# Expert loop of a mixture-of-experts layer: token rows gathered from HBM in every pass, or picked from SBUF in every second one

## The chip, the cores and the metric

The kernel runs on one core of one Trainium2 chip. The metric is the device time of one execution in microseconds. TensorE, VectorE, ScalarE, GpSimd and SyncE are called PE, DVE, ACT, POOL and SP, as in the profile.

## What is computed

The program is a two-layer decoder trunk on 512 tokens of width 1024. Each layer has a token mixer (layer 0 a forgetting attention, layer 1 an RWKV-7 recurrence), beside it a cross-attention into a memory, and then a mixture of experts with a residual and a layer norm. The change touches only the mixture of experts, which runs once in each layer:

```python
scores = sigmoid(x2 @ w_router)
_, idx = top_k(scores + router_bias, 6)           # 6 of 64 experts for each of 512 tokens
gate = renormalised scores of those six * 2.5
for each expert e:                                # xb: the rows of x2 whose idx names e
    hb = silu(xb @ w_gate[e]) * (xb @ w_up[e])    # 1024 -> 256
    yb = hb @ w_down[e]                           # 256 -> 1024
    acc[tok] += yb * gate
```

So 3072 (token, expert) rows of 4 KB go through 64 experts, whose weights are 3 matrices of 1 MB each. Everything is float32.

## The kernel before, in words

`routed_experts_tables` computes the routing of a layer. It leaves in SBUF the rank of every token within every expert (`K.rank`), columns from which token numbers can be computed (`K.slot_cols`), and a plan: experts are taken two by two, a pair at a time, and each pair gets one pass with 64 slots for either expert, or more passes where an expert has more than 64 tokens. It also stores the layer's activations X (512 x 1024, which stay resident in SBUF too) to HBM as `x_rows` (L278).

`expert_loop` (from L468) is the loop over passes. Every engine runs its own loop; the bodies are written out for the pass numbers of even and odd parity (`u` or `s`, 0 and 1), since most buffers are double. The first two passes stand ahead of the loop (L524). What the engines do for pass n:

- DVE makes a one-hot matrix of token against slot in bfloat16, [128 tokens, 4 token tiles, 128 slots], by comparing ranks with slot numbers (`one_hot`, L532), four passes ahead.
- PE multiplies it with `slot_cols` (`slot_rows`, L540, three passes ahead), which gives the token number of each of the 128 slots. DVE turns it into an index column (`index_rows`, L550).
- POOL starts an indirect DMA, the gather, with that column. It brings 128 rows of 4 KB from `x_rows` into `xg[s]`; indexes of empty slots are out of bounds and move nothing (`gather`, L560). It is issued two passes ahead, once PE has turned the rows that were in the buffer.
- PE transposes the gathered rows in 8 blocks of 128x128, `turn_x` (L568), into banks 0 and 1. ACT and DVE copy one bank each into `xt[s]` (`keep_xt`, L576). This is done one pass ahead, between the gate/up products and the down products.
- PE makes the gate and up products, 64 matmuls with 256 columns, 64 slots of one expert in either half of the array (`gate_up`, L584). ACT and DVE compute the hidden values (L598, L603), PE turns them (L609), DVE keeps them (L616).
- PE makes the down products, 16 matmuls with 512 columns (`down`, L620). ACT and DVE copy the result (L633), and POOL scatters its rows to `y_rows` in HBM (L642).

PE's order within a pass stands in `from_slot` (L710): `gate_up(n)`, `turn_x(n+1)`, `turn_h(n)`, `slot_rows(n+3)`, `down(n)`.

The weights have two slots, each for one pair of experts. SP refills a slot as soon as the last pass of its pair has finished with a matrix (`refill`, L654): the next gate matrices (2 x 1 MB) after the gate products, then up, then down. All these loads stand in one queue, in order. `gate_up` waits at its start for both the gate and the up matrices of its pair (L586), `down` for the down matrices (L621).

Of the kernel before, what the change touches and what calls it, by code (L numbers as in the profile page):

```python
# [7 lines left out]
F32, BF16, I32, U32 = mybir.dt.float32, mybir.dt.bfloat16, mybir.dt.int32, mybir.dt.uint32  # L8
ALU, ACT, AX = mybir.AluOpType, mybir.ActivationFunctionType, mybir.AxisListType

P = 128
D = 1024
T = 512
NT = T // P
KD = D // P
# [68 lines left out]
def wait_from(eng, sem, value):  # L84

    if not (isinstance(value, int) and value <= 0):
        eng.wait_ge(sem, value)
# [380 lines left out]
def expert_loop(K, L, shared, out=None, next_weights=None):  # L468
# [6 lines left out]
    nc, B, ident = K.nc, K.banks, K.ident  # L475
    with Phase(nc) as scope:
        def sb(name, shape, dt=F32):
            return scope.enter_context(nc.sbuf_tensor(f"{name}{L}", shape, dt))

        def sem(name):  # L480
            return scope.sem(f"experts{L}_{name}")

        xt_room = K.XT[:].rearrange("p k t -> p (k t)")
        onehot = [sb(f"onehot{s}", [P, NT, 2, SLOTS], BF16) for s in range(2)]
        tok_f = [sb(f"tok_f{s}", [P, 1]) for s in range(2)]
        tok = [sb(f"tok{s}", [P, 1], I32) for s in range(2)]
        ahead = [sb(f"ahead{s}", [P, 3], I32) for s in range(2)]
        row = [sb(f"row{s}", [P, 1], I32) for s in range(2)]
        xg = [xt_room[:, s * D:(s + 1) * D] for s in range(2)]
        xt = [xt_room[:, (2 + s) * D:(3 + s) * D].rearrange("p (k t) -> p k t", k=KD) for s in range(2)]  # L490
        y = [sb(f"y{s}", [P, D]) for s in range(2)]
        sig, gu, h = sb("sig", [P, FE]), sb("gu", [P, FE]), sb("h", [P, FE])
        ht = sb("ht", [P, 2, P])
        ending = Combination(K, L, scope, shared, out, next_weights)
        slots = B[4][:, 0:4]
        gate, up = B[2][:, 0:FE], B[7][:, 0:FE]

        cleared = sem("cleared")
        onehot_made, slots_made, index_made = sem("onehot_made"), sem("slots_made"), sem("index_made")
        gathered = [sem("gathered0"), sem("gathered1")]  # L500
        x_turned, xt_a, xt_d = sem("x_turned"), sem("xt_a"), sem("xt_d")
        gate_done, gate_up_done, sigmoid_done, hidden_done = sem("gate_done"), sem("gate_up_done"), sem("sigmoid_done"), sem("hidden_done")
        h_turned, ht_kept, down_done = sem("h_turned"), sem("ht_kept"), sem("down_done")
# [4 lines left out]
        def entry(eng, table, n, most):  # L508

            return eng.value_load(table[0:1, bass.ds(n, 1)] if not isinstance(n, int) else table[0:1, n:n + 1],  # L510
                                  min_val=0, max_val=most)

        def through(n, s):

            return 8 * (n - s) + 16

        def held(eng, value):

            return value if isinstance(value, int) else eng.to_reg(value)  # L520

        def loop(eng, body):

            for u in range(2):  # L524
                body(u, u)
            turns = eng.value_load(K.plan_turns[0:1, 0:1], min_val=PAIRS // 2, max_val=MAX_PASSES // 2)
            with eng.Fori(1, turns) as turn:
                for u in range(2):
                    body(turn * 2 + u, u)

        def one_hot(dve, s, n):  # L532
            pair, level = entry(dve, K.plan_pair, n, PAIRS - 1), entry(dve, K.plan_level, n, EXTRA)
            for t in range(NT):
                last = dve.tensor_tensor(  # L535
                    onehot[s][:, t], K.rank[:, t, bass.ds(pair * 2, 2)].unsqueeze(2).to_broadcast([P, 2, SLOTS]),
                    K.iota_s[:, bass.ds(level * SLOTS, SLOTS)].unsqueeze(1).to_broadcast([P, 2, SLOTS]), ALU.is_equal)
            last.then_inc(onehot_made, 1)
# [10 lines left out]

        def index_rows(dve, s, dst, n, step):  # L550
            dve.wait_ge(slots_made, n + 1)
            wait_from(dve, gathered[s], through(n - 2, s))
            step(dve.tensor_scalar(tok_f[s][:], slots[:, 0:1], float(NOBODY), slots[:, 1:2], ALU.add, ALU.add))
            dve.tensor_copy(tok[s][:], tok_f[s][:])
            for a in range(2):
                half = slice(64 * a, 64 * a + 64)
                last = dve.tensor_tensor(dst[half, :], slots[half, 2 + a:3 + a], tok_f[s][half, :], ALU.add)
            last.then_inc(index_made, 1)

        def gather(pool, s, n):  # L560
            value = held(pool, n + 1)
            pool.wait_ge(cleared, 1)
            pool.wait_ge(index_made, value)
            pool.indirect_dma_start(out=xg[s], out_offset=None, in_=K.x_rows,  # L564
                                    in_offset=bass.IndirectOffsetOnAxis(ap=tok[s][:], axis=0),
                                    bounds_check=T - 1, oob_is_err=False).then_inc(gathered[s], 16)

        def turn_x(pe, s, n):  # L568
            pe.wait_ge(gathered[s], through(n, s))
            xk = xg[s].rearrange("p (q k) -> p k q", k=KD)  # L570
            for k in range(KD):
                ins = pe.transpose(B[k // 4][:, (k % 4) * P:(k % 4 + 1) * P], xk[:, k, :], ident[:])  # L572
                if k % 4 == 3:
                    ins.then_inc(x_turned, 1)
# [41 lines left out]
        def keep_ht(dve, n):  # L616
            dve.wait_ge(h_turned, n + 1)
            dve.tensor_copy(ht[:].rearrange("p j t -> p (j t)"), B[3][:, 0:2 * P]).then_inc(ht_kept, 1)  # L618
# [23 lines left out]
        def scatter(pool, s, n):  # L642
            value = held(pool, n + 1)
            pool.wait_ge(cleared, 1)
            pool.wait_ge(y_a, value)
            pool.wait_ge(y_d, value)
            pool.indirect_dma_start(out=K.y_rows, out_offset=bass.IndirectOffsetOnAxis(ap=row[s][:], axis=0),  # L647
                                    in_=y[s][:], in_offset=None,
                                    bounds_check=TOPK * T - 1, oob_is_err=False).then_inc(stored[s], 16)

        with nc.Block() as block:
# [24 lines left out]

            @block.gpsimd
            def _(pool):
                pool.memset(xg[0], 0.0)  # L679
                pool.memset(xg[1], 0.0).then_inc(cleared, 1)  # L680
                pool.wait_ge(cleared, 1)
                gather(pool, 0, 0)
                gather(pool, 1, 1)

                def one_pass(n, u):
                    read = held(pool, 2 * (n + 1))
                    pool.wait_ge(cleared, 1)
                    pool.wait_ge(x_turned, read)
                    gather(pool, u, n + 2)
                    scatter(pool, u, n)  # L690

                loop(pool, one_pass)
                turns = pool.value_load(K.plan_turns[0:1, 0:1], min_val=PAIRS // 2, max_val=MAX_PASSES // 2)
                all_stored, all_gathered = held(pool, turns * 16), held(pool, turns * 16 + 16)
                for s in range(2):
                    pool.wait_ge(cleared, 1)
                    pool.wait_ge(stored[s], all_stored)
                    pool.wait_ge(gathered[s], all_gathered)
                pool.memset(tok_f[0][:], 0.0).then_inc(ending.y_stored, 1)

            @block.tensor
# [35 lines left out]
            @block.vector  # L737
            def _(dve):
                step = Chain(dve, steps)
                one_hot(dve, 0, 0)  # L740
                one_hot(dve, 1, 1)
                for n in range(3):
                    index_rows(dve, n % 2, ahead[1][:, n:n + 1], n, step)
                    if n < 2:
                        one_hot(dve, n % 2, n + 2)
                keep_xt(dve, 0, 0, 1)
                start = step.n

                def one_pass(n, u):
                    step = Chain(dve, steps, start + n * PASS_STEPS)  # L750
                    hidden(dve, n, step)
                    keep_xt(dve, 1 - u, n + 1, 1)
                    keep_ht(dve, n)

                    wait_from(dve, stored[u], through(n - 2, u))
                    dve.wait_ge(index_made, n + 3)
                    dve.tensor_copy(row[u][:], ahead[1 - u][:, 0:1])
                    dve.tensor_copy(ahead[u][:, 0:2], ahead[1 - u][:, 1:3])
                    index_rows(dve, 1 - u, ahead[u][:, 2:3], n + 3, step)
                    one_hot(dve, u, n + 4)  # L760
                    keep_y(dve, u, n, 1)

                loop(dve, one_pass)
                ending.sums(dve)
# [1744 lines left out]
```

## Time and profile before

| | us |
|---|---|
| median of 3 runs | 2351.93 |
| lowest, highest | 2348.82, 2356.43 |
| the profiled execution | 2349.78 |
| its span, first to last instruction | 2348.0 |

In the profiled execution PE was busy for 85% of the span, DVE for 35%, ACT for 15% and POOL for 12%. The two expert loops lie at about 453 to 999 us and 1726 to 2284 us of the span. The mean granted TensorE clock was 0.912 of full speed (the two levels are 1.2 and 2.4 GHz, shown as 0.5 and 1.0).

How to read it: times are microseconds unless marked ns. A row of a timeline gives start, length, engine, line, operation, what it writes and reads, and in square brackets how long the engine had been idle before, and what released it. "PEld" are the weight loads of PE, which overlap its matmuls. "xt room" buffers (`xg` and `xt`) show in the profile as XT.

### The profile page before, as it was taken

The numbers are of one execution on the slowest core, as the hardware profiler recorded it, in microseconds if no ns is written. First come the engines' busy times: TensorE is split into PE (matmuls) and PEld (weight loads), VectorE is DVE, ScalarE is ACT, GpSimd is POOL, SyncE is SP. The second block draws the span as 40 slices with busy tenths as digits, with TensorE's granted clock in tenths as the row PEclk, the third lists the DMA queues.
The fourth block names the chain that finished last, engine by engine and source line by source line (L and its number), as shares of the span: only waits on it lengthen the run. The fifth ranks groups of instructions, "written<-read, shape, count | busy, mean of one in ns | idle before, by whom it ended". The sixth has DMA issues, their size and how long they took to land. (4 is left out here: it accounts for less than half of the span.)

```text
span 2348.0 us, 33222 instructions
## 1 busy us (share of the span) xinstructions
PE 2004.9 (85%) x11180; PEld 1226.0 (52%) x11181; DVE 828.0 (35%) x2198; ACT 361.7 (15%) x814; POOL 289.8 (12%) x375
## 2 busy tenths in 40 slices
PE   8999998798989887878897688988779897888885
PEld 5475545365655555533444377763446564554552
DVE  2001645422223222272545743313523232222236
ACT  1001631011101100012334211110101010100010
POOL 5000000011111111100134131000011111111110
PEclk9999999799989999998998599879889899998998
DMA  6211003699999999861222100002758999999966
GB/s 210 77 54 39 34 19 151 239 365 421 414 418 379 412 421 421 347 232 50 59 54 50 23 2 1 1 1 90 284 188 326 421 395 410 412 421 421 417 279 250
DMA packets 143456, 540.51 MB, mean 230 GB/s; under 512 B 30854, under 2 KB 68286, under 8 KB 93590
## 3 DMA queue, kind: packets, MB, share of 16 engines
q1 hardware_dynamic: 122070, 489.14, 52.0%
q0 software_dynamic: 21312, 50.37, 5.7%
q8 instruction: 48, 0.79, 0.1%
q14 instruction: 26, 0.21, 0.0%
HBM read 521.07 MB, written 45.61 MB: 241 GB/s over the span
## 5 line engine op out<-in xcount | busy, mean ns | idle before, releaser
L594 PE MATMUL bank<-W,XT 128*64 128x256 f32 x4608 | 569.1, 409 | 116.2 <-DMA W<-in_w_exp_up_dram 108.0
L594 PEld LDWEIGHTS bank<-W,XT 128*64 128x64 f32 x4608 | 413.2, 148 | 296.7 <-issue 197.9
L629 PE MATMUL bank<-W,ht 128*64 128x512 f32 x1152 | 263.1, 597 | 12.2 <-DVE ht L618 12.0
L647 POOL DMA_INDIRECT y_rows<-y,row x72 | 72.9, 1013 | 943.1 <-DVE y L640 943.1
L605 DVE TENSOR_TENSOR gu<-sig,bank 128x256 f32<-128x256 f32 x72 | 30.4, 422 | 409.5 <-ACT sig L601 409.5
L1733 PE MATMUL bank<-XT,rin_w 128*128 128x512 f32 x352 | 161.5, 615 | 0.0
L629 PEld LDWEIGHTS bank<-W,ht 128*64 128x64 f32 x1152 | 90.9, 136 | 127.0 <-issue 127.0
L1087 PE MATMUL bank<-XT,foxw 128*128 128x512 f32 x320 | 139.9, 599 | 0.0
L1733 PEld LDWEIGHTS bank<-XT,rin_w 128*128 128x128 f32 x352 | 68.6, 198 | 88.7 <-issue 88.4
L535 DVE TENSOR_TENSOR onehot<-rank,iota_s 128x128 bf16 x320 | 71.9, 287 | 97.9 <-issue 97.9
L601 ACT ACTIVATE sig<-bank 128x256 f32<-128x256 f32 x72 | 27.7, 384 | 508.5 <-PE bank L594 508.5
L1087 PEld LDWEIGHTS bank<-XT,foxw 128*128 128x128 f32 x320 | 61.4, 193 | 76.4 <-issue 76.4
L607 DVE TENSOR_TENSOR h<-gu,bank 128x256 f32<-128x256 f32 x72 | 30.4, 422 | 193.2 <-PE bank L594 193.2
L580 ACT ACTIVATE XT<-bank 128x512 f32<-128x512 f32 x74 | 44.2, 597 | 339.6 <-PE bank L572 339.6
L572 PE MATMUL bank<-ident,XT 128*128 128x128 f32 x592 | 87.3, 291 | 3.9 <-DMA XT<-x_rows,tok 3.9
L572 PEld LDWEIGHTS bank<-ident,XT 128*128 128x128 f32 x592 | 72.9, 195 | 31.8 <-issue 27.7
L1475 PE MATMUL bank<-w_out,XT 128*128 128x512 f32 x192 | 82.8, 593 | 1.5 <-PEq L80 1.5
L564 POOL DMA_INDIRECT XT<-x_rows,tok x76 | 77.6, 1021 | 39.7 <-issue 26.1
L638 ACT ACTIVATE y<-bank 128x512 f32<-128x512 f32 x72 | 43.0, 597 | 215.9 <-PE bank L629 215.9
L640 DVE COPY y<-bank 128x512 f32<-128x512 f32 x72 | 49.8, 692 | 72.4 <-PE bank L629 72.4
L545 PE MATMUL bank<-slot_cols,onehot 128*128 x312 | 43.5, 176 | 32.4 <-issue 15.5
L679 POOL MEMSET XT<- 128x1024 f32 x2 | 1.9, 956 | 545.4 <-POOLq L80 545.4
(390 smaller groups left out, 2395.9 us busy)
## 6 DMA issues: line engine op xcount, KB each, us to landing
W<-in_w_exp_gate_dram SPq DMA_DIRECT2D x128, 1024.0 KB, 14.6
W<-in_w_exp_up_dram SPq DMA_DIRECT2D x128, 1024.0 KB, 19.2
W<-in_w_exp_down_dram SPq DMA_DIRECT2D x128, 1024.0 KB, 17.9
W<-y_rows SPq DMA_DIRECT2D x16, 1536.0 KB, 17.6
foxw<-in_fox_w_in_dram SPq DMA_DIRECT2D x13, 1024.0 KB, 5.5
rin_w<-in_rwkv_w_in_dram SPq DMA_DIRECT2D x22, 512.0 KB, 4.0
w_out<-in_w_out_dram SPq DMA_DIRECT2D x1, 4096.0 KB, 13.2
x_rows<-X SPq DMA_DIRECT2D x2, 2048.0 KB, 16.4
```

Of the source, the lines that this page charges most:

```text
L535: last = dve.tensor_tensor(onehot[s][:, t], K.rank[:, t, bass.ds(pair * 2, 2)].unsqueeze(2).to_broadcast([P, 2, SLOTS]), K.iota_s[:, bass. ...
L545: last = pe.matmul(slots, onehot[s][:, t].rearrange("p a s -> p (a s)"), K.slot_cols[:, t, bass.ds(pair, 1), :].rearrange("p i c -> p (i c)"),
L564: pool.indirect_dma_start(out=xg[s], out_offset=None, in_=K.x_rows, in_offset=bass.IndirectOffsetOnAxis(ap=tok[s][:], axis=0), bounds_chec ...
L572: ins = pe.transpose(B[k // 4][:, (k % 4) * P:(k % 4 + 1) * P], xk[:, k, :], ident[:])
L580: eng.activation(dst, B[0][:], ACT.Copy).then_inc(xt_a, 1)
L594: last = pe.matmul((gate, up)[m][64 * a:64 * a + 64, :], xt[s][:, k, 64 * a:64 * a + 64], K.W[:, w, a, m, k * FE:(k + 1) * FE], start=(k = ...
L629: last = pe.matmul(B[5 + half][64 * a:64 * a + 64, :], ht[:, j, 64 * a:64 * a + 64], K.W[:, w, a, 2, at:at + 512], start=(j == 0), stop=(j ...
L640: eng.tensor_copy(dst, B[6][:]).then_inc(y_d, 1)
L647: pool.indirect_dma_start(out=K.y_rows, out_offset=bass.IndirectOffsetOnAxis(ap=row[s][:], axis=0), in_=y[s][:], in_offset=None, bounds_ch ...
L1087: last = pe.matmul(bank[:], wc[n % NB][:, k, o * P:(o + 1) * P], K.XT[:, k, :], start=(k == 0), stop=(k == KD - 1))
L1475: last = pe.matmul(B[4 + i % 4][:], K.XT[:, k, t * P:(t + 1) * P], w[:, k, n * 512:(n + 1) * 512], start=(k == 0), stop=(k == KD - 1))
L1733: last = pe.matmul(main(i)[:], wc[i % WBUFS][:, kb, :], K.XT[:, kb, :], start=(kb == 0), stop=(kb == KD - 1))
```

## The change

Passes of odd number no longer gather. In their place PE picks the token rows out of X: for each of 8 column blocks it accumulates 4 products (one for each token tile) of X's block as the stationary operand with the one-hot matrix as the moving one, which gives directly what the 8 transposes gave, the block of columns turned, in the same places of banks 0 and 1. For that, DVE copies the one-hot matrix of every odd pass from bfloat16 into a float32 tile `hot` after `keep_ht` of each even pass. The index column and the float32 token numbers of odd passes are still made, since the scatter needs them; the int32 copy that only the gather used is not. `xg` and `tok` become single buffers.

```diff
-        tok = [sb(f"tok{s}", [P, 1], I32) for s in range(2)]
+        tok = sb("tok", [P, 1], I32)
-        xg = [xt_room[:, s * D:(s + 1) * D] for s in range(2)]
+        xg = xt_room[:, 0:D]
+        hot = sb("hot_rows", [P, NT, P])
...
         def one_hot(dve, s, n):
             pair, level = entry(dve, K.plan_pair, n, PAIRS - 1), entry(dve, K.plan_level, n, EXTRA)
+            if s:
+                wait_from(dve, hot_made, n - 1)
...
         def index_rows(dve, s, dst, n, step):
             dve.wait_ge(slots_made, n + 1)
-            wait_from(dve, gathered[s], through(n - 2, s))
+            if s == 0:
+                wait_from(dve, gathered, through(n - 2, s))
             step(dve.tensor_scalar(tok_f[s][:], slots[:, 0:1], float(NOBODY), slots[:, 1:2], ALU.add, ALU.add))
-            dve.tensor_copy(tok[s][:], tok_f[s][:])
+            if s == 0:
+                dve.tensor_copy(tok[:], tok_f[s][:])
...
+        def keep_hot(dve, n):
+            dve.wait_ge(onehot_made, n + 1)
+            dve.tensor_copy(hot[:], onehot[1][:].rearrange("p t a s -> p t (a s)")).then_inc(hot_made, 2)
+
+        def pick_x(pe, n):
+            pe.wait_ge(hot_made, n + 1)
+            for k in range(KD):
+                for t in range(NT):
+                    ins = pe.matmul(B[k // 4][:, (k % 4) * P:(k % 4 + 1) * P], K.Xk[:, t, k, :], hot[:, t, :],
+                                    start=(t == 0), stop=(t == NT - 1))
+                if k % 4 == 3:
+                    ins.then_inc(x_turned, 1)
+
         def turn_x(pe, s, n):
-            pe.wait_ge(gathered[s], through(n, s))
-            xk = xg[s].rearrange("p (q k) -> p k q", k=KD)
+            if s:
+                return pick_x(pe, n)
+            pe.wait_ge(gathered, through(n, s))
+            xk = xg.rearrange("p (q k) -> p k q", k=KD)
...
             def _(pool):
-                pool.memset(xg[0], 0.0)
-                pool.memset(xg[1], 0.0).then_inc(cleared, 1)
+                pool.memset(xg, 0.0).then_inc(cleared, 1)
                 pool.wait_ge(cleared, 1)
-                gather(pool, 0, 0)
-                gather(pool, 1, 1)
+                gather(pool, 0)
 
                 def one_pass(n, u):
-                    read = held(pool, 2 * (n + 1))
-                    pool.wait_ge(cleared, 1)
-                    pool.wait_ge(x_turned, read)
-                    gather(pool, u, n + 2)
+                    if u == 0:
+                        read = held(pool, 2 * (n + 1))
+                        pool.wait_ge(cleared, 1)
+                        pool.wait_ge(x_turned, read)
+                        gather(pool, n + 2)
                     scatter(pool, u, n)
...
                 for n in range(3):
                     index_rows(dve, n % 2, ahead[1][:, n:n + 1], n, step)
+                    if n == 1:
+                        keep_hot(dve, 1)
...
                     keep_xt(dve, 1 - u, n + 1, 1)
                     keep_ht(dve, n)
+                    if u == 0:
+                        keep_hot(dve, n + 3)
```

## Rows read from the trace of the kernel before

**Rows 1.** Waits of PE over the whole span: total us, times, longest

```profile
PE bank L594 <- DMA W<-in_w_exp_up_dram: 108.0, 39, 4.4
PE bank L594 <- issue: 6.4, 4, 2.8
```

**Rows 2.** Stretches of time: both loops first; clock, DMA share and GB/s stand last

```profile
core 0: us, PE busy (x) PEld busy (x) DVE busy (x) ACT busy (x) POOL busy (x), PEclk, DMA share, GB/s
453.00:999.42 546.42, 477.77 (x3384) 309.22 (x3384) 148.65 (x539) 57.86 (x112) 71.84 (x71) 0.95 0.96 394
1725.60:2284.45 558.85, 484.78 (x3384) 309.21 (x3384) 148.71 (x539) 57.89 (x112) 71.87 (x71) 0.94 0.93 383
2049.00:2187.00 138.00, 114.28 (x754) 70.73 (x756) 33.27 (x120) 12.64 (x24) 15.43 (x16) 0.90 1.02 421
2118.00:2122.00 4.00, 4.00 (x22) 2.61 (x24) 0.00 (x0) 0.00 (x0) 1.12 (x2) 0.58 1.02 424
2122.00:2127.00 5.00, 5.00 (x47) 3.40 (x43) 0.56 (x2) 0.38 (x1) 0.00 (x0) 1.00 1.01 419
1660.00:1665.40 5.40, 5.39 (x32) 5.20 (x30) 2.08 (x3) 2.20 (x4) 0.00 (x0) 0.63 0.72 228
```

**Rows 3.** Timeline of PE in the second loop: a pass with a long wait, then one without

```profile
1873.41 9.86 PE L594 MATMUL bank<-W,XT 128*64 128x256 f32 x64 [3.79 <-DMA W<-in_w_exp_up_dram]
...
1888.99 7.11 PE L594 MATMUL bank<-W,XT 128*64 128x256 f32 x64
1896.03 1.16 PE L572 MATMUL bank<-ident,XT 128*128 128x128 f32 x8
1897.02 0.40 PE L613 MATMUL bank<-ident,h 128*128 128x128 f32 x2
1897.67 0.55 PE L545 MATMUL bank<-slot_cols,onehot 128*128 x4 [0.25 <-issue]
1898.38 3.65 PE L629 MATMUL bank<-W,ht 128*64 128x512 f32 x16 [0.16 <-DVE ht L618]
1901.83 7.11 PE L594 MATMUL bank<-W,XT 128*64 128x256 f32 x64
```

**Rows 4.** Timeline of PE: gate/up products of two passes that follow each other

```profile
2049.12 8.81 PE L594 MATMUL bank<-W,XT 128*64 128x256 f32 x64 [3.90 <-DMA W<-in_w_exp_up_dram]
...
2066.49 8.81 PE L594 MATMUL bank<-W,XT 128*64 128x256 f32 x64 [2.63 <-DMA W<-in_w_exp_up_dram]
```

**Rows 5.** DMA queues from 2049 to 2187 us: packets, MB, share of 16 engines

```profile
q1 hardware_dynamic: 7147, 52.05, 90.4%
q0 software_dynamic: 2304, 6.11, 11.2%
```

**Rows 6.** Timeline of SP: the first refills of gate matrices in the second loop

```profile
1731.09 0.87 SPq L465 DMA_DIRECT2D W<-in_w_exp_gate_dram  x2
...
1757.53 0.86 SPq L465 DMA_DIRECT2D W<-in_w_exp_gate_dram  x2
...
1787.89 0.86 SPq L465 DMA_DIRECT2D W<-in_w_exp_gate_dram  x2
```

**Rows 7.** Timeline of PE: float32 products in the RWKV layer, and transposes of X

```profile
1493.52 6.05 PE L2145 MATMUL bank<-W 128*128 128x128 f32 x48
...
1659.57 5.83 PE L293 MATMUL bank<-ident,X 128*128 128x128 f32 x32 [7.26 <-PEq L80]
```

**Rows 8.** Groups by line and shape: count, busy us, mean ns, idle us

```profile
L1087 PE MATMUL bank<-XT,foxw 128*128 128x512 f32 x320 | 139.9, 599 | 0.0
L564 POOL DMA_INDIRECT XT<-x_rows,tok x76 | 77.6, 1021 | 39.7 <-issue 26.1 <-PE bank L572 7.2 <-DVE ahead L557 6.4
L618 DVE COPY ht<-bank 128x256 f32<-128x256 f32 x72 | 29.9, 415 | 0.0
```

**Rows 9.** Timeline of DVE in the pass that starts at 1875 us

```profile
1887.38 0.90 DVE L535 TENSOR_TENSOR onehot<-rank,iota_s 128x128 bf16 x4 [1.21 <-issue]
...
1889.23 0.69 DVE L640 COPY y<-bank 128x512 f32<-128x512 f32 x1 [0.95 <-PE bank L629]
```

More of the change, by code:

```diff
@@ L499, in expert_loop @@
         onehot_made, slots_made, index_made = sem("onehot_made"), sem("slots_made"), sem("index_made")
-        gathered = [sem("gathered0"), sem("gathered1")]
+        gathered, hot_made = sem("gathered"), sem("hot_made")
         x_turned, xt_a, xt_d = sem("x_turned"), sem("xt_a"), sem("xt_d")
@@ L558, in index_rows, with gather @@
             last.then_inc(index_made, 1)
-        def gather(pool, s, n):
+        def gather(pool, n):
             value = held(pool, n + 1)
@@ L563, in gather @@
             pool.wait_ge(index_made, value)
-            pool.indirect_dma_start(out=xg[s], out_offset=None, in_=K.x_rows,
-                                    in_offset=bass.IndirectOffsetOnAxis(ap=tok[s][:], axis=0),
-                                    bounds_check=T - 1, oob_is_err=False).then_inc(gathered[s], 16)
+            pool.indirect_dma_start(out=xg, out_offset=None, in_=K.x_rows,
+                                    in_offset=bass.IndirectOffsetOnAxis(ap=tok[:], axis=0),
+                                    bounds_check=T - 1, oob_is_err=False).then_inc(gathered, 16)
+        def keep_hot(dve, n):
[9 more added lines that the diff above has]
+                    ins.then_inc(x_turned, 1)
         def turn_x(pe, s, n):
-            pe.wait_ge(gathered[s], through(n, s))
-            xk = xg[s].rearrange("p (q k) -> p k q", k=KD)
+            if s:
+                return pick_x(pe, n)
+            pe.wait_ge(gathered, through(n, s))
+            xk = xg.rearrange("p (q k) -> p k q", k=KD)
             for k in range(KD):
@@ L697, in _ @@
                     pool.wait_ge(stored[s], all_stored)
-                    pool.wait_ge(gathered[s], all_gathered)
+                pool.wait_ge(gathered, all_gathered)
                 pool.memset(tok_f[0][:], 0.0).then_inc(ending.y_stored, 1)
```

## The prediction

> **What bounds the kernel now.** I began with the waits of PE, because PE is the busiest engine. In both layers together its gate/up products wait 39 times, 108.0 us in all, for the matrices of a pair (the last, up, is the one named); everything else that they wait for is 6.4 us [rows 1]. Next the stretches: DMA is 93 to 96% busy over the two loops, and 100% busy at 421 GB/s from 2049 to 2187 us [rows 2]. So the loop has two bounds that lie close together. Where nothing is late, a pass is PE alone: from 1888.99 to 1901.83 us, 12.84 us [rows 3]. Where every pair has one pass, the period is the weight stream's: 17.37 us from one start to the next [rows 4], 17.2 in the mean, since the 138 us from 2049 to 2187 hold 754/94 = 8 passes of 94 PE instructions [rows 2]. Those waits cost twice: the gate/up products behind one take 8.8 to 9.9 us, not 7.1 [rows 3, 4], since the granted clock is at its lower level, 1.2 GHz, for a while after the idle time (0.58 in the first 4 us, 1.00 in the next 5 [rows 2]).
>
> A loop has 36 passes (3384 = 36 x 94 PE instructions [rows 2]) for 32 pairs. Four pairs have two passes. They show as passes in which SP issues no gate refill: in the second loop nothing between 1731.09 and 1757.53, nor from there to 1787.89 us, where a pass is some 13 us long [rows 6]. There DMA gets ahead and PE then runs some passes without a wait. The 36 full-speed passes are 462 us; the loops take 546.4 and 558.8 us (the first two stretches of [rows 2]).
>
> **The change, part by part.** Picks: 18 in each loop (for passes 1, 3, ... 35), 32 products in place of 8 transposes, in PE's own order between gate/up and turn_h, so each lengthens PE's part of an even pass. The 8 transposes go at (1.16 - 0.28)/7 = 126 ns apiece [rows 3]. Real float32 products of the same shape, 128x128 by 128 columns, go at (6.05 - 0.28)/47 = 123 ns [rows 7]. I take 126 ns: 24 more are **3.0 us a pick**, 54 us a loop, 109 us in both. Bounds: below, the moving columns alone, 512 columns in 139.9/320 = 437 ns [rows 8], so 109 ns for 128, which is 2.6 us a pick; above, the only 32 products that have the tile X itself as stationary operand, 5.83 us [rows 7], so 5.83 - 1.16 = 4.7 us a pick. I stay with 3.0, because that row ran at a granted clock of 0.63 [rows 2] and the picks run behind gate/up products at full clock.
>
> Gathers: 19 fewer in each loop, one of them for a pass past the end, without rows. Gathers and scatters had 11.2% of the 16 engines' time in 138 us of 8 passes [rows 5], 0.97 us for one of the two. Where the weight stream binds, each gather that goes gives back about 0.95 us, at most 17 us a loop. Bounds: nothing, if the stream of weights runs no faster without it (then the total is a rival, below); above, 1.1 us.
>
> POOL loses 38 issues of 1.0 us [rows 8]; it is mostly idle, so they cost nothing now. The scatter of an odd pass no longer stands behind a gather; nobody is waiting for it before the end.
>
> DVE gets one copy of 512 columns bfloat16 to float32 in an even pass. No such row exists; 256 columns out of PSUM take 415 ns [rows 8], so 0.3 to 0.7 us. It stands behind keep_ht and ahead of index_rows, one_hot and keep_y. Ahead of keep_y DVE has 0.95 us idle, and 1.21 ahead of one_hot [rows 9]; even late, keep_y is wanted by PE only at the next pass's down products, 10 us on. The slot product of the next pass waits for index_rows, again a pass away. Cost 0; without that cover at most 18 x 0.7 = 13 us a loop. The one-hot matrix it copies was made a pass earlier, and the pick that read `hot` last has ended before keep_ht. The waits on hot_made are then past. The tok copy on odd passes (150 ns) goes, off the path.
>
> **The sum.** PE at full speed becomes 462 + 54 = 516 us a loop, below the 546 and 559 of now; what decides is how much waiting is left. I stepped the 36 passes of each loop through a replay with these rules. PE: gate/up 7.04 us, then 1.1 (transposes; 4.1 for a pick), 1.05 to the down products, 3.65 for these [rows 3]; if the wait ahead was over 2.05 us, gate/up takes 1.7 more, over 3.5 us, 2.7 more [rows 3, 4]. The weights: 2.10 MB in order for gate, up and down, released at the middle and the end of gate/up and the end of down of a pair's last pass, there 2 us after the last byte. Gather and scatter 0.38 MB each, beside them at half the rate (6.11 MB in 16 of them [rows 5]). Pairs with two passes are pairs 1, 2, 7 and 13 of the second loop and 2, 8, 14 and 20 of the first, counted from 0, as the missing refills show. The starting stalls (first gate/up, code fetches) as they are. The one free number, the DMA rate, is 0.4075 MB/us (421 GB/s measured), set so that the kernel before comes out: 545.8 and 560.4 us against 546.4 and 558.8.
>
> With picks and without odd gathers the replay gives 538.2 and 553.8 us: -7.6 and -6.6, **-14 us** together. By its parts, second loop: 516.6 at full speed, 23.6 waits (67.9 before), 12.0 lower clock (28.3 before), 1.6 start. In words: up to the last pair with two passes hardly a wait is left, since PE needs 14.35 us a pass in the mean and the stream 16.7; in the final run of single pairs the stream still binds, and each two passes shrink by one gather. The extra PE work of 109 us is nearly all paid by waits and half-clock products that it replaces.
>
> Against the profiled execution's 2349.8 us that is 2336; the median of the runs is 2 us higher, so I say 2338. Price of a pick: 2.6 us gives -15, 3.4 -7, 3.8 +4, 4.6 +20. DMA rate 0.400 or 0.415: -13 and -6. A measurement of this kernel tells about 0.3%, 7 us, from no change.
>
> **Rivals.** (1) PE becomes the bound: a pick costs clearly more than 24 x 126 ns, by its stationary loads from X with a stride of 32 bytes, or by accumulating four times into one place. From 3.7 us a pick on, the gain is gone; at 4.6 the replay gives +20, 2372 us. For it: the X row of 5.83 us [rows 7]. Against: its clock, and that the turned tile xg has the same stride at 126 ns. 15%. (2) The gather is no relief: weights come no faster without it (rows of 4 KB fill gaps of the stream). Then the replay with gathers kept gives +14, 2366 us; 12%. For it: the two queues' shares add to 101.6% [rows 5], so engine time may be counted while both wait. Against: 421 GB/s in all whatever the mix. (3) In between: either price half as bad, -7 to +7, 2345 to 2358; 20%. (4) PE stays warm and the stream is faster than I think: all weight waits go, both loops go to 518 to 523 us, -60, 2292; 5%. (5) The gathers on odd passes don't go, or the picks wait for `hot`: nothing in the code says so; under 2%.
>
> The forecast, 8 to 24 us faster, has 46%. The range reaches from 2322 to 2366 and so leaves out the far part of (1) and (4). Faster by over 0.3%: 0.51 (the forecast and rival 4); within: 0.22 (3 and 5); slower: 0.27 (1 and 2). The likeliest case alone: 2328 to 2344.
>
> **What would show it.** Right: picks as 36 groups of 32 at 4.0 to 4.1 us; PE's waits for up matrices down from 108 us to 35 to 45, in fewer than 20 places, almost all in the last third of each loop; software queue down from 50 MB to about 38; PEclk over the loops up from 0.95 and 0.94 to 0.97 or more; loops of about 539 and 553 us; nothing else in the span moved. Wrong: a pick over 4.7 us; a period of single pairs still at 17.2 us (then the gather was no relief); PE waiting for `hot` or for DVE's copies; issue gaps of over 1 us inside the loop.

## The result, and the profile after

Before and after were run by turns on one chip: before 2351.19 us (median of 4 runs, 2348.82 to 2356.43), after **2708.69 us** (median of 4, 2703.43 to 2718.7). The ratio is 1.152, 95% interval 1.148 to 1.156: 357 us slower. The forecast was 2338 us and the range ended at 2366, so both were wrong, and so was the sign that had the highest chance. The profiled execution of after took 2703.43 us, with a span of 2701.7.

From the page of the changed kernel: busy time of the engines, PE's clock over the span, the DMA queues, the shares of the chain that ended last, and the groups of the picks (line 581) and of the gate/up products (line 614, line 594 of before):

```profile
PE 2451.4 (91%) x13196; PEld 1724.0 (64%) x13197; DVE 836.1 (31%) x2198; ACT 361.1 (13%) x814; POOL 248.4 (9%) x335
...
PEclk9998998999999999998997688798899999999998
...
q1 hardware_dynamic: 122070, 489.14, 46.1%
q0 software_dynamic: 15840, 37.58, 3.7%
...
PE 26%; DVE 2%; issue 1%; DMA 1%; DVEq 0%; ACT 0%; POOLq 0%; SPq 0%
...
L581 PEld LDWEIGHTS bank<-hot_rows,X 128*128 128x128 f32 x2304 | 552.6, 336 | 13.8 <-issue 13.8
L581 PE MATMUL bank<-hot_rows,X 128*128 128x128 f32 x2304 | 559.5, 404 | 0.0
L614 PE MATMUL bank<-W,XT 128*64 128x256 f32 x4608 | 520.3, 383 | 8.2 <-issue 6.5
```

One group holds the result: the picks keep PE busy for 559.5 us, where some 150 (36 picks of 4.1) were forecast. The number of their records (a record is one instruction in the profile) is the first clue. The source has 36 x 32 = 1152 products and the profile 2304 records. In the chain that ended last DMA has 1% of the span, where it had 11% before. The software queue moves 37.58 MB, as forecast ("down to about 38").

The waits of PE over the whole span answer to [rows 1]:

```profile
PE bank L649 <- issue: 29.0, 34, 0.9
...
PE bank L649 <- DVE ht L638: 7.7, 38, 0.9
...
PE bank L614 <- issue: 6.5, 2, 3.5
```

No row for a wait of the gate/up products for their matrices is left; before they waited 39 times, 108.0 us. The 29.0 us of issue are one gap of up to 0.86 us in 34 of the 36 passes with a pick, ahead of their down products. They are no new cost: in the passes of the timeline below, from the start of turn_h (line 633) to the start of the down products is 1.34 us where the rows were gathered and 1.33 where they were picked (the down products behind that pick start at 562.23); only the slot products in between end sooner.

Both loops, in the columns of [rows 2]:

```profile
core 0: us, PE busy (x) PEld busy (x) DVE busy (x) ACT busy (x) POOL busy (x), PEclk, DMA share, GB/s
450.86:1180.94 730.08, 704.66 (x4392) 559.25 (x4392) 152.43 (x539) 57.83 (x112) 53.18 (x53) 0.99 0.72 288
1904.48:2638.00 733.52, 707.69 (x4392) 558.14 (x4392) 152.54 (x539) 57.81 (x112) 53.10 (x53) 0.99 0.71 283
```

DMA is busy for 0.72 and 0.71 of the loops at 288 and 283 GB/s, where it was 0.96 and 0.93 at 394 and 383. No product waits for its weights any longer; PE has become the only bound. The two loops together take 1463.6 us against 1105.3, 358.3 more; the span grew by 353.7, so the rest of it is 4.6 us shorter. PE is busy for 449.8 us more in them (1412.35 against 962.55) and idle for 91.5 us less. Last the timeline of PE, a pass with a gather and then one with a pick, against [rows 3]:

```profile
525.65 7.11 PE L614 MATMUL bank<-W,XT 128*64 128x256 f32 x64
532.69 1.16 PE L592 MATMUL bank<-ident,XT 128*128 128x128 f32 x8
533.68 0.40 PE L633 MATMUL bank<-ident,h 128*128 128x128 f32 x2
534.30 0.57 PE L548 MATMUL bank<-slot_cols,onehot 128*128 x4 [0.21 <-issue]
535.02 3.65 PE L649 MATMUL bank<-W,ht 128*64 128x512 f32 x16 [0.16 <-DVE ht L638]
538.48 7.11 PE L614 MATMUL bank<-W,XT 128*64 128x256 f32 x64
545.51 15.55 PE L581 MATMUL bank<-hot_rows,X 128*128 128x128 f32 x64
560.90 0.39 PE L633 MATMUL bank<-ident,h 128*128 128x128 f32 x2
561.13 0.24 PE L548 MATMUL bank<-slot_cols,onehot 128*128 x4
562.23 3.65 PE L649 MATMUL bank<-W,ht 128*64 128x512 f32 x16 [0.86 <-issue]
```

From start to start the eight transposes take 0.99 us and a pick 15.39: **14.4 us more a pick, not 3.0**. 36 x 14.4 = 518 us of new work for PE. PE is busy for only 449.8 us more, 68 less than that. Gate/up products make up 48.8 of the 68: they fell from 569.1 to 520.3 us in all, since few of them run at the lower level of the clock (1.2 GHz) now (granted clock 0.99 over the loops, 0.95 and 0.94 before). The slot products give 11.5 (43.5 to 32.0 us); the down products rose by 6.7 (263.1 to 269.8). The remaining 15 us or so are not taken apart: rows that follow closely overlap at their ends, so the sums of groups and the busy time of PE differ.

The pick's time holds two factors. It has 64 records, where 32 had been counted. And each stands for (15.55 - 0.40)/63 = 240 ns of PE's time, where 126 had been taken. The group names a suspect for the second: its loads of the stationary operand take 336 ns, where the loads of the transposes (line 572 of before) take 195.

### The profile page after: what moved, and what is told of

Its sections match the earlier page's. It is cut to its first block and busy times, and to the rows that moved or that the text cites. A ratio compares the mean times of both kernels' runs of the same rounds, so it can differ in the third digit from the quotient of the medians.

```text
span 2701.7 us, 37068 instructions
## 1 busy us (share of the span) xinstructions
PE 2451.4 (91%) x13196; PEld 1724.0 (64%) x13197; DVE 836.1 (31%) x2198; ACT 361.1 (13%) x814; POOL 248.4 (9%) x335
## 3 DMA queue, kind: packets, MB, share of 16 engines
q0 software_dynamic: 15840, 37.58, 3.7%
## 5 line engine op out<-in xcount | busy, mean ns | idle before, releaser
L581 PEld LDWEIGHTS bank<-hot_rows,X 128*128 128x128 f32 x2304 | 552.6, 336 | 13.8 <-issue 13.8
L581 PE MATMUL bank<-hot_rows,X 128*128 128x128 f32 x2304 | 559.5, 404 | 0.0
L614 PE MATMUL bank<-W,XT 128*64 128x256 f32 x4608 | 520.3, 383 | 8.2 <-issue 6.5
L614 PEld LDWEIGHTS bank<-W,XT 128*64 128x64 f32 x4608 | 400.6, 139 | 144.1 <-issue 51.6
L649 PE MATMUL bank<-W,ht 128*64 128x512 f32 x1152 | 269.8, 610 | 36.8 <-issue 29.0
L602 DVE COPY XT<-bank 128x512 f32<-128x512 f32 x74 | 51.1, 691 | 563.5 <-PE bank L581 539.3
L625 DVE TENSOR_TENSOR gu<-sig,bank 128x256 f32<-128x256 f32 x72 | 30.3, 421 | 249.3 <-ACT sig L621 232.7
L627 DVE TENSOR_TENSOR h<-gu,bank 128x256 f32<-128x256 f32 x72 | 30.3, 421 | 188.4 <-PE bank L614 188.4
L1498 PEld LDWEIGHTS bank<-w_out,XT 128*128 128x128 f32 x192 | 36.4, 190 | 47.8 <-issue 47.8
L307 PE MATMUL bank<-XT,w_sh 128*128 128x512 f32 x128 | 60.0, 626 | 0.0
```

The costliest lines, as they stand in the source:

```text
L307: last = pe.matmul(B[gu * 2 + j][:], w_sh[:, gu, k * FE + j * P:k * FE + (j + 1) * P], XT[:, k, :], start=(k == 0), stop=(k == KD - 1))
L581: ins = pe.matmul(B[k // 4][:, (k % 4) * P:(k % 4 + 1) * P], K.Xk[:, t, k, :], hot[:, t, :], start=(t == 0), stop=(t == NT - 1))
L602: eng.tensor_copy(dst, B[1][:]).then_inc(xt_d, 1)
L614: last = pe.matmul((gate, up)[m][64 * a:64 * a + 64, :], xt[s][:, k, 64 * a:64 * a + 64], K.W[:, w, a, m, k * FE:(k + 1) * FE], start=(k = ...
L649: last = pe.matmul(B[5 + half][64 * a:64 * a + 64, :], ht[:, j, 64 * a:64 * a + 64], K.W[:, w, a, 2, at:at + 512], start=(j == 0), stop=(j ...
L1498: last = pe.matmul(B[4 + i % 4][:], K.XT[:, k, t * P:(t + 1) * P], w[:, k, n * 512:(n + 1) * 512], start=(k == 0), stop=(k == KD - 1))
```

## The experiments

Eight more kernels ran. The price of a pick is always read from start to start in the timeline of PE, and the transposes' 0.99 us is taken off. Changes are against the kernel before on the same chip: 2349.64 us (11 runs) for the first four, 2350.2 (23) for the next two, 2352.14 (11) for the last two. "The replay" is the prediction's recurrence with only the price of a pick, or the gathers, put in anew. With 14.4 us it gives +352.6 (loops of 730.0 and 728.7 us, against 730.08 and 733.52 measured). It is good to a few us only: at 2.6 us a pick it gave -15 in the prediction and gives -16 below.

### 1. The same products, stationary blocks without a stride

```diff
-                    ins = pe.matmul(B[k // 4][:, (k % 4) * P:(k % 4 + 1) * P], K.Xk[:, t, k, :], hot[:, t, :],
+                    ins = pe.matmul(B[k // 4][:, (k % 4) * P:(k % 4 + 1) * P], K.X[:, t, k * P:(k + 1) * P], hot[:, t, :],
```

The columns of X come out in another order than the weight rows want; the number and the shape of the products stay.

> The changed kernel, but each pick product reads 128 neighbouring columns of X as its stationary operand in place of every eighth column (so the picked columns are in another order than the gate and up matrices want; the work on every engine is the same). Theory 'stride': a record of a pick costs 240 ns and not 123 because its stationary block is read with a step of 32 bytes. Then the 64 records go at 123 ns, a pick is 7.9 us, 6.9 more than the 8 transposes, and by the replay the kernel is 83 us slower than before, about 2433 us. Rival 'accumulation or the one-hot operand': the step is nothing, a pick stays at 15.4 us and the time at about 2705 us.

Measured: 2415.37 us (2 runs), ratio 1.028 [1.025, 1.030], 66 us slower than before instead of 357. A pick on PE's timeline, and its two groups:

```profile
2005.48 7.41 PE L581 MATMUL bank<-hot_rows,X 128*128 128x128 f32 x64
```

```profile
L581 PEld LDWEIGHTS bank<-hot_rows,X 128*128 128x128 f32 x2304 | 260.0, 192 | 13.8 <-issue 13.8
L581 PE MATMUL bank<-hot_rows,X 128*128 128x128 f32 x2304 | 266.8, 277 | 0.0
```

Still 64 records, now at 113 ns, with loads of 192 ns instead of 336. The rival (accumulation or the one-hot operand) falls. The expected size was too large: 123 ns a record and 83 us were expected. A pick is 7.25 us, 6.3 more than the transposes; the replay gives +62.6 with that. So the stride costs 8.1 us a pick and the second record the larger part of what is left. A real float32 product of this shape takes 2 x 113 = 227 ns.

### 2. 32 transposes in place of the products

```diff
-                    ins = pe.matmul(B[k // 4][:, (k % 4) * P:(k % 4 + 1) * P], K.Xk[:, t, k, :], hot[:, t, :],
-                                    start=(t == 0), stop=(t == NT - 1))
+                    ins = pe.transpose(B[k // 4][:, (k % 4) * P:(k % 4 + 1) * P], K.Xk[:, t, k, :], ident[:])
```

The same stationary blocks with the same stride; what reaches the products is the last token tile turned, not the picked rows. The waits on the one-hot matrix stay.

> The changed kernel with 32 transposes of the same strided blocks of X in place of the 32 pick products (each overwrites the one before; what odd passes compute is not what the reference wants). This is the price that the prediction took: one record of 126 ns for each, 4.0 us a pick. If the prediction's replay was right and only the price of a pick was wrong, the time is 14 us below the kernel before (2337 us), with about 24 and 14 us of waits for weights left in the loops. Rival 'the gathers were no relief': 14 us above it (2365 us). Theory 'stride' in its strong form (any strided read of X is slow, a transpose too): 240 ns each, 7.7 us, and about 80 us slower.

Measured: 2336.7 us (8 runs, 2326.35 to 2344.65), ratio 0.994 [0.992, 0.996], 13 us faster than before. A pick, and the loads:

```profile
2018.17 3.81 PE L581 MATMUL bank<-ident,X 128*128 128x128 f32 x32
```

```profile
L581 PEld LDWEIGHTS bank<-ident,X 128*128 128x128 f32 x1152 | 131.4, 193 | 13.9 <-issue 13.9
```

32 transposes are 32 records at 114 ns, 3.65 us a pick and 2.66 more than eight. That is the price the prediction put down, and the time it forecast from it (2338; the replay gives -16.6). The waits for matrices fall to the forecast's place too:

```profile
PE bank L613 <- DMA W<-in_w_exp_up_dram: 35.2, 19, 3.1
```

35.2 us in 19 places, where 35 to 45 in fewer than 20 were forecast; the granted clock over the loops is 0.98 (0.97 or more was forecast). With the price of 24 more transposes in place of a real product's, the rest of the prediction holds in this run, to a few us. It also shows no burden of the stride on a transpose: 193 ns a load and 114 a record, at the same 32 bytes that make them 336 and 240 for a product. No contiguous block was transposed in this place.

The Trainium skill ("TensorE: Matmul & The Clock Gate", Terms) calls the transpose mode four times faster for FP32. Here that is so only against the strided product (481 ns against 114); against the contiguous one it is twice (227 against 114).

One thing blurs the time of this run:

```profile
PE bank L613 <- issue: 12.9, 2, 10.5
```

10.5 us of that are one wait ahead of the third pass, for no cause that the profile shows. Runs 1, 5 and 7 have one such wait of 8.0 to 9.3 us there or a pass later; in the kernel before the longest is 2.8. The eight times of this run lie 18 us apart, and how much of that is this wait stays open.

### 3. No rows at all in odd passes

Odd passes neither gather nor pick: PE turns eight blocks of a cleared tile, at the price of before. The computation of these rows is left out.

```diff
+        still = xt_room[:, D:2 * D].rearrange("p (q k) -> p k q", k=KD)
...
+            pe.wait_ge(cleared, 1)
             pe.wait_ge(hot_made, n + 1)
             for k in range(KD):
-                for t in range(NT):
-                    ins = pe.matmul(B[k // 4][:, (k % 4) * P:(k % 4 + 1) * P], K.Xk[:, t, k, :], hot[:, t, :],
-                                    start=(t == 0), stop=(t == NT - 1))
+                ins = pe.transpose(B[k // 4][:, (k % 4) * P:(k % 4 + 1) * P], still[:, k, :], ident[:])
...
+                pool.memset(xt_room[:, D:2 * D], 0.0)
```

> The kernel before without the gathers of odd passes and without picks: odd passes turn 8 blocks of a cleared tile, so their rows are left out; the one-hot copy on DVE stays. It measures what the gathers that go are worth alone. The replay: 30 us faster than before (2321 us; 17 and 14 us in the two loops), by a period of 16.7 us in single pairs in place of 17.2. Rival 'no relief, the weight stream is as fast with the gathers beside it': no change, 2351 us.

Measured: 2321.22 us (4 runs), ratio 0.987 [0.985, 0.990], 28 us faster. Two gate/up products, ten passes apart, where every pair has one pass:

```profile
2060.96 7.13 PE L614 MATMUL bank<-W,XT 128*64 128x256 f32 x64 [1.35 <-DMA W<-in_w_exp_up_dram]
...
2227.66 7.13 PE L614 MATMUL bank<-W,XT 128*64 128x256 f32 x64 [1.35 <-DMA W<-in_w_exp_up_dram]
```

A period is 166.7/10 = 16.67 us (16.7 was expected), against 17.2: half a gather less in each pass, 0.53 us a pass, so a gather is worth about 1.1 us of the stream where 0.95 was taken. In time the replay has -30 for this kernel against -28 measured. The gathers are the relief that the prediction said; rival 2 (no relief) falls. 28 us is also all that the odd gathers can give. What a pick adds on PE is set against that, and by the replay the gain is gone once a pick takes about 4.7 us (3.7 more than the transposes).

### 4. One token tile of the four

```diff
-                for t in range(NT):
-                    ins = pe.matmul(B[k // 4][:, (k % 4) * P:(k % 4 + 1) * P], K.Xk[:, t, k, :], hot[:, t, :],
-                                    start=(t == 0), stop=(t == NT - 1))
+                ins = pe.matmul(B[k // 4][:, (k % 4) * P:(k % 4 + 1) * P], K.Xk[:, 0, k, :], hot[:, 0, :],
+                                start=True, stop=True)
```

Tokens of the other three tiles are left out. Rival 1 named two causes of a dear pick, the strided loads and "accumulating four times into one place"; here nothing is accumulated and the stride stays.

> The changed kernel with the picks' products of the first token tile alone: 8 products, 16 records, nothing accumulated, three quarters of the tokens left out. Theory 'stride': still 240 ns a record, 3.9 us for a pick, 2.9 more than the transposes, so by the replay 14 us faster than before (2337 us). Rival 'accumulation': 123 ns a record, 2.0 us, and 26 us faster (2325 us).

```profile
2017.53 4.08 PE L580 MATMUL bank<-hot_rows,X 128*128 128x128 f32 x16
```

Sixteen records for 8 products, 4.08 us: (4.08 - 0.40)/15 = 245 ns each, as with accumulation. So the accumulation is free, and with run 1 the stride is the whole factor between 113 and 240 ns a record. The time is 2329.1 us (3 runs), ratio 0.991 [0.989, 0.993], 21 us faster; the replay gives -14 for 2.9 us more a pick. The 7 us between them are not explained; this run has none of the long waits of run 2 (its longest wait on issue is 3.1 us).

### 5. Both halves of X in bfloat16

The experiments leave a way to keep the change: bfloat16 products, with X split into a high and a low half, some 16 bits of its mantissa together. The halves are made at the start of each layer's loop (ACT rounds, POOL subtracts), in contiguous blocks; `hot` becomes bfloat16. They share their room with the ending's diagonal and norm weights, so the norm weights are loaded later.

```diff
...
+            pe.wait_ge(x_rest, 8)
             for k in range(KD):
                 for t in range(NT):
-                    ins = pe.matmul(B[k // 4][:, (k % 4) * P:(k % 4 + 1) * P], K.Xk[:, t, k, :], hot[:, t, :],
-                                    start=(t == 0), stop=(t == NT - 1))
+                    for part in (xhi, xlo):
+                        ins = pe.matmul(B[k // 4][:, (k % 4) * P:(k % 4 + 1) * P], part[:, t, k, :], hot[:, t, :],
+                                        start=(t == 0 and part is xhi), stop=(t == NT - 1 and part is xlo))
...
```

> A version that is to beat both kernels. Before the loop ACT copies X block by block, neighbouring columns, to bfloat16 and POOL makes the bfloat16 of what is left (X minus that); a pick is 64 products, both halves of X's block as contiguous bfloat16 stationary operands against a bfloat16 one-hot matrix, so 64 records as in the changed kernel, and picked rows carry some 16 bits of X. For room, the diagonal and the layer norm's weights of the loop's ending share the tile of the halves, and these weights are loaded after the first result rows. Theory 'two records of a float32 product, doubled by the step of 32 bytes': a bfloat16 record with a contiguous block goes at 58 ns or so (the pace of the four bfloat16 weight loads of a slot product behind a pick, 0.27 us), a pick is 3.8 to 4.0 us, and the replay gives -14 us, 2337. Rival 'a weight load of 128 columns takes 113 ns in any type': a pick is 7.3 us and the kernel about 65 us slower than before, as with contiguous float32 blocks.

```profile
2010.32 3.75 PE L586 MATMUL bank<-XT,x_halves 128*128 128x128 bf16 x64
```

```profile
PE bank L619 <- DMA W<-in_w_exp_up_dram: 37.5, 19, 3.1
...
PE bank L551 <- DVE ahead L565: 30.3, 4, 13.5
```

A bfloat16 product is one record of 57 ns, a quarter of the contiguous float32 product's 227. That agrees with the Trainium skill ("FP8 and Floating Point Precision", TensorE Precision Notes: true FP32 takes four passes). A pick is 3.58 us and the weight waits are as forecast, yet the kernel takes 2357.6 us (12 runs), ratio 1.003 [1.002, 1.005], where 2337 was expected. The second wait row holds the loss: 13.5 us in one place. The timeline of DVE there, and that of POOL beside it:

```profile
443.70 12.44 DVE L541 TENSOR_TENSOR onehot<-rank,iota_s 128x128 bf16 x4 [1.02 <-issue]
```

```profile
445.03 10.75 POOL L710 TENSOR_TENSOR x_halves<-X,x_halves 128x512 bf16<-128x512 f32 x8
```

DVE's four one-hot operations take 0.90 us elsewhere and 12.44 here, ending right after POOL's subtractions. The first passes' indices wait for them: over both loops PE waits 30.3 us for them, where the changed kernel has 7.6, and the first gate/up products start at 460.37 us (450.86 in the changed kernel, 453.02 before, 454.8 to 455.3 in runs 1, 2 and 4). This is what the Trainium skill says of the two engines ("GPSIMD Engine Reference", Specifications: shared SBUF interfaces, contention with DVE instructions that have two SBUF inputs), and here its price is 11.5 us for four small operations; run 7, where POOL no longer subtracts, bears it out.

### 6. The high half alone

As 5 with half the products: X is rounded to bfloat16 in the picked rows. POOL's subtractions are left in.

```diff
-                    for part in (xhi, xlo):
-                        ins = pe.matmul(B[k // 4][:, (k % 4) * P:(k % 4 + 1) * P], part[:, t, k, :], hot[:, t, :],
-                                        start=(t == 0 and part is xhi), stop=(t == NT - 1 and part is xlo))
+                    ins = pe.matmul(B[k // 4][:, (k % 4) * P:(k % 4 + 1) * P], xhi[:, t, k, :], hot[:, t, :],
+                                    start=(t == 0), stop=(t == NT - 1))
```

> The same with the upper half alone (32 bfloat16 products a pick; picked rows are X rounded to bfloat16). If a record goes at about 58 ns a pick is 1.9 us, 0.9 more than the transposes, and the replay gives -27 us, 2323; at 113 ns a pick is 3.6 us, and -16 us, 2334. The difference to the kernel with both halves is the price of 32 records.

Measured: 2347.88 us (10 runs), ratio 0.999 [0.998, 1.001]. A pick is 1.80 us; with 0.8 us more than the transposes the kernel is 10 us faster than run 5, and it misses its expected time, 2323 us, by 25, most of it at the start of the loops again (30.4 us of waits there, one of 13.5).

### 7. The low half made on DVE

```diff
...
-                        pool.wait_ge(x_kept, 2 * t + g + 1)
-                        pool.tensor_tensor(xlo[:, t, 4 * g:4 * g + 4, :], K.Xk[:, t, 4 * g:4 * g + 4, :],
+                        dve.tensor_tensor(xlo[:, t, 4 * g:4 * g + 4, :], K.Xk[:, t, 4 * g:4 * g + 4, :],
                                            xhi[:, t, 4 * g:4 * g + 4, :], ALU.subtract).then_inc(x_rest, 1)
...
```

The subtractions move behind DVE's copy for the first pass. The norm weights are loaded one tile of rows later.

> The version with both bfloat16 halves, mended where its two costs showed: the lower half is made by DVE in the 5 us that it idles behind the first rows' copy, not by POOL, beside which a one-hot comparison of DVE took 12.4 us in place of 0.9 at the start of either loop (the first gate/up product started at 460.4 us and not at 450.9); and the layer norm's weights are loaded one tile of result rows later. A pick stays at 3.6 us, 2.6 more than the transposes, for which the replay gives -16 us. Theory 'the gain of the picks was eaten by the start and the end alone': the first gate/up product is back at about 451 us, and the time is 2334 to 2340 us, 10 to 16 below the kernel before. Rival 'the picks themselves gain nothing beyond single runs': within 5 us of the kernel before.

Measured: **2338.72 us** (6 runs, 2328.3 to 2340.92), ratio 0.994 [0.992, 0.996]: faster than both kernels. DVE at the start of the loop:

```profile
446.27 0.93 DVE L541 TENSOR_TENSOR onehot<-rank,iota_s 128x128 bf16 x4 [1.02 <-issue]
...
453.59 8.02 DVE L779 TENSOR_TENSOR x_halves<-X,x_halves 128x512 bf16<-128x512 f32 x8
```

The one-hot operations are back at 0.9 us, and the first gate/up products start at 453.70 us (about 451 was expected). The pick is the same 64 records of run 5, so the 19 us that this run gains on run 5 are the start of the loops and the changed load together. At the first gate/up products of the second loop 13.8 us of them are there (1719.67 us against 1733.45); the rest was not taken apart. This is the change as it was meant, at the forecast's time.

### 8. The high half in every pass, no gathers

Every pass picks its rows by 32 bfloat16 products; the gathers, their indices and the tile they land in are gone. All rows of X that the experts see are rounded to bfloat16. Against the kernel before, from POOL's loop:

```diff
...
-                    read = held(pool, 2 * (n + 1))
-                    pool.wait_ge(cleared, 1)
-                    pool.wait_ge(x_turned, read)
-                    gather(pool, u, n + 2)
                     scatter(pool, u, n)
...
```

> Every pass picks its rows, by 32 bfloat16 products from the upper half alone (picked rows are X rounded to bfloat16), and no pass gathers. A pick costs 0.8 us more than 8 transposes; 76 gathers go, with 25 MB. The replay, with the same rules, gives 36 passes of 13.65 us on PE against a stream that needs 16.2 us for a single pair: -48 us, about 2302. Rival 'once the odd gathers are gone, the even ones no longer cost the stream anything': no better than the -25 us that the replay gives for the high half in odd passes alone, 2325.

Measured: **2288.36 us** (4 runs), ratio 0.972 [0.970, 0.974], 64 us faster than before. Waits, and two gate/up products ten passes apart:

```profile
PE bank L628 <- DVE ht L617: 48.3, 72, 0.8
PE bank L593 <- DMA W<-in_w_exp_up_dram: 39.9, 23, 2.3
```

```profile
2046.54 7.13 PE L593 MATMUL bank<-W,XT 128*64 128x256 f32 x64 [1.69 <-DMA W<-in_w_exp_up_dram]
...
2191.02 7.13 PE L593 MATMUL bank<-W,XT 128*64 128x256 f32 x64 [2.32 <-DMA W<-in_w_exp_up_dram]
...
2207.04 8.81 PE L593 MATMUL bank<-W,XT 128*64 128x256 f32 x64 [2.19 <-DMA W<-in_w_exp_up_dram]
```

The 48.3 us behind `ht` are the 0.67 us in each pass between the picks' slot products and the down products; like the gap of the changed kernel they are no new cost. The period of single pairs is 160.5/10 = 16.05 us: 17.2 with a gather in each pass, 16.67 with one in two, 16.05 with none. Of the 23 waits for matrices 18 are followed by gate/up products at full clock (7.13 us), even behind the longest, 2.32 us (the row of 2191.02); five are followed by 8.7 to 8.8 us. Expected were 48 us less; the rest, some 16 us, is only in part explained. The loops are 6 us each shorter than the replay has them (530.3 against 536.2 for the second). It charges the lower clock behind each wait of over 2.05 us, where six in ten of these passes don't pay it, and it has 16.2 us for the period. The remaining 4 us are open; they are not won at the start, since the first gate/up products come at 453.19 us, as before (453.02). No run separates these.

## Why the prediction was wrong, point by point

The changes in us of five kernels, by the replay with the measured price of a pick, and as measured:

| run | pick over transposes, us | replay | measured |
|---|---|---|---|
| transposes (2) | 2.7 | -17 | -13 |
| one tile, strided (4) | 2.9 | -14 | -21 |
| halves on DVE (7) | 2.6 | -16 | -13 |
| contiguous float32 (1) | 6.3 | +63 | +66 |
| the change | 14.4 | +353 | +357 |

**The step that failed is one term: "24 more are 3.0 us a pick".** It measured 14.4. Three readings led to it. First, the x48 of [rows 7] was taken for 48 products, at 123 ns. The code at that line (six rounds of four heads) has 24 products: a float32 product is written as two pairs of load and product, a transpose as one. The same count stood in [rows 3]: gate/up has 2 x 8 x 2 = 32 products in the source and x64 in the row, down 8 and x16 (so the "64 matmuls" and "16 matmuls" in the description of the kernel before are records too). Read so, the row gives 246 ns a product and a pick of 7.9 us, close to run 1 (7.25 us, 66 us slower than before).

Second, from this misreading came "The trace doesn't agree: 123 ns" on the four passes of the Trainium skill ("FP8 and Floating Point Precision", TensorE Precision Notes). The trace did agree, at 246 ns. By that rule the prediction had 5.8 us more a pick and 49 us in all; run 1, without the stride, measured 6.3 and 66. It was the nearest number in the prediction, and it got no chance of its own.

Third, both bounds (2.6 and 4.7 us) hung on the same misreading. The lower one divided a row that counts records as well (x320 of 512 columns). The upper one was taken from 32 transposes at a low clock, which says nothing of a product. The stride was named in rival 1, and dismissed "since the turned tile xg has the same stride at 126 ns". Run 2 shows why that fails: a transpose of a strided block is as fast as ever, and only a real float32 product pays, 240 ns a record and not 113. None of the rows that the prediction rests on had that combination, so none could exclude it; the range should have been open above.

**Gathers: right.** 0.95 us each was taken, 1.1 as the bound above. Run 3 gives about 1.1 us in the period, and -28 for all of them against -30 by the replay.

**POOL and DVE at nothing: right.** PE never waits for `hot`, the copy takes 0.42 us, and runs 2 and 7 come out at the forecast with it in place.

**Waits and lower clock paid back: right.** In run 2 the waits are down to 35.2 us of 108. In the changed kernel they are gone altogether, and give back 91.5 us of idle time and 68 of PE's busy time (48.8 of it gate/up products) against the 518 added. Once they are used up, each further microsecond of a pick costs 36 at once; that is why +3 us costs nothing and +14.4 costs 357. The rule that the lower clock follows a wait of over 2.05 us is rough: before, the products at 552.74 us take 7.13 us behind a wait of 2.97.

**The rivals.** Rival 1 (PE becomes the bound) came true, by the stride that it names, at three times its last price of 4.6 us. Rival 2 falls with run 3, and rival 3 with the result. Rival 4 falls with run 2: 35.2 us of weight waits stay. Run 8 comes near its 2292 us by another way, with no gathers left. Rival 5 falls too, since half of the gathers went and PE has no wait for `hot`.

## What to carry to other kernels

Before a group's time is divided by its count, divide the count by the source: if a float32 product shows as two records, the price of a product is twice that of the row, and a transpose of the same shape is no measure for it. When a rule of the Trainium skill and a row differ by just such a factor, test the reading of the row first, and let the rule keep its chance. Work given to an engine that waits is free only up to what it waits (here 108 us of waits and some 50 of slow gate/up products), so a one-hot product in place of a gather has to be cheap in cycles (bfloat16 halves, contiguous stationary blocks), not just off the DMA queue.

## What the runs showed of the hardware

- A stationary float32 block read at a step of 32 bytes costs a real product 240 ns a record and not 113 (loads of 336 and 192 ns; the changed kernel and run 1). The same strided block in a transpose takes 114 ns, with loads of 193 (run 2).
- 128x128 by 128 columns at full clock: a contiguous bfloat16 product 57 ns (run 5), a strided float32 transpose 114 (run 2), a contiguous float32 product 227 (run 1), a strided one 481.
- Eight POOL subtractions of two SBUF operands (10.75 us) stretched DVE's four one-hot operations from 0.9 to 12.4 us. On DVE the same eight took 8.0 (run 7).
- Ahead of the same stream of weights, the period of a pair fell by 0.53 and then 0.62 us as gathers went from one a pass to one in two and to none.
